# Mixer of a two-layer encoder kernel: jobs in another order, sixteen gate columns kept in DRAM

## The reference, cut to what matters

```python
for layer in range(2):
    xn = rmsnorm(h, mix_norm_g[layer])
    hq, hf, hi, hg, aq, ak, av, iq, ik, iw, gate_a, gate_b = split(xn @ w_in[layer])
    y_a = hgrn2_mixer(hq, hf, hi, hg, ...)       # 4 heads of 128, gated recurrence
    y_b = dsa_mixer(aq, ak, av, iq, ik, iw, ...) # 8 heads of 64, the best 132 keys of each query
    merged = sigmoid(gate_a) * (y_a @ w_branch_hgrn) + sigmoid(gate_b) * (y_b @ w_branch_dsa)
    h = h + merged @ w_out[layer]
    h = h + hier_moe(rmsnorm(h, ...))            # top-1 group, top-2 of its experts
return rmsnorm(h, final_norm_g)[:, 16:]
```

## Time and profile before

| what | value |
|---|---|
| median of three runs | 2030.24 us (2028.77 to 2033.95) |
| the profiled execution, its own time | 2032.07 us |
| its span | 2030.4 us |
| mean granted clock of TensorE | 0.845 of full speed |
| PE busy | 1575.7 us (78%) |
| DVE, ACT, POOL busy | 754.5, 543.2, 472.7 us |
| HBM read and written | 296.00 and 31.72 MB |

### The profile page before, as it was taken

How to read it: one execution, slowest core, us unless ns; L and a number is a source line. 1 busy time by engine, 2 the same in 40 slices (tenths; PEclk the granted TensorE clock), 3 DMA queues, 4 the chain that set the end, 5 groups by cost and what they waited for, 6 DMA issues and landing times.

```text
span 2030.4 us, 31814 instructions
## 1 busy us (share of the span) xinstructions
PE 1575.7 (78%) x11236; PEld 1193.3 (59%) x11236; DVE 754.5 (37%) x1772; ACT 543.2 (27%) x988; POOL 472.7 (23%) x349
## 2 busy tenths in 40 slices
PE   2998569967998597777459976799689986978771
PEld 2778349944976454444247863698379674545440
DVE  3018777944041311101241287696432223110103
ACT  3235432235221021111222444330543120111111
POOL 5312642100440010010143236230105101110002
PEclk9999559969998599989779975699589976999995
DMA  4224001210144199999832120011105343999995
GB/s 155 83 83 166 2 1 43 84 42 1 66 178 182 64 354 377 385 383 379 287 115 75 51 84 2 1 64 63 42 1 191 115 167 118 370 383 383 385 394 172
DMA packets 90628, 329.47 MB, mean 162 GB/s; under 512 B 10832, under 2 KB 11216, under 8 KB 73600
## 3 DMA queue, kind: packets, MB, share of 16 engines
q1 hardware_dynamic: 67536, 267.89, 35.2%
q0 software_dynamic: 9344, 33.95, 5.2%
q10 hardware_dynamic: 13616, 25.90, 3.6%
HBM read 296.00 MB, written 31.72 MB: 161 GB/s over the span
## 4 chain that ended last, share of the span: by engine, by line
PE 44%; issue 16%; SPq 15%; DMA 10%; DVE 8%; POOL 4%; ACT 3%; ACTq 0%; DVEq 0%; POOLq 0%
PE ps L585 14%; PE ps L608 12%; SPq L482 10%; SPq L487 4%; PE ps L850 4%; DMA gu_ring<-w_expert_up 3%; PE ps L595 3%; DMA r<-w_expert_up 3%; POOL gate_up_low L1754 2%; PE ps L776 2%; PE ps L871 2%; DMA r<-yrow,sidx 1%; PE ps L808 1%; PE ps L769 1%; PE ps L752 1%
## 5 line engine op out<-in xcount | busy, mean ns | idle before, releaser
L1754 POOL TENSOR_TENSOR gate_up_low<-gu_ring,chunk_high_a 128x1024 fp32r<-128x1024 f32 x80 | 193.1, 2434 | 531.6 <-ACT chunk_high_a L1486 531.6
L608 PE MATMUL ps<-x_high,gate_up_low 128*128 128x264 f32 (+1 forms) x928 | 265.5, 286 | 0.0
L608 PE MATMUL ps<-x_high,chunk_high_a 128*128 128x264 f32 x896 | 255.7, 285 | 3.5 <-POOL gate_up_low L1754 3.2
L608 PE MATMUL ps<-x_low,chunk_high_a 128*128 128x264 f32 x896 | 254.4, 284 | 0.0
L1817 POOL DMA_INDIRECT r<-xrow,idx x64 | 57.0, 890 | 663.0 <-PE ps L839 445.8
L608 PEld LDWEIGHTS ps<-x_high,gate_up_low 128*128 128x128 f32 (+1 forms) x928 | 173.4, 187 | 0.7
L850 PE MATMUL ps<-gu_ring,r 128*64 128x256 f32 x1024 | 131.3, 414 | 54.2 <-DMA gu_ring<-w_expert_up 52.9
L608 PEld LDWEIGHTS ps<-x_high,chunk_high_a 128*128 128x128 f32 x896 | 168.3, 188 | 5.4 <-issue 5.4
L608 PEld LDWEIGHTS ps<-x_low,chunk_high_a 128*128 128x128 f32 x896 | 168.5, 188 | 0.0
L585 PE MATMUL ps<-gate_up_low,x_high 128*128 128x512 f32 (+1 forms) x400 | 159.1, 398 | 0.0
L1388 DVE COPY r<-ps 128x512 f32<-128x512 f32 x64 | 44.2, 691 | 298.3 <-PE ps L839 298.3
(11 more groups left out here) (295 smaller groups left out, 3094.3 us busy)
## 6 DMA issues: line engine op xcount, KB each, us to landing
gu_ring<-w_in SPq DMA_DIRECT2D x20, 2048.0 KB, 8.3
gu_ring<-w_expert_gate SPq DMA_DIRECT2D x32, 1024.0 KB, 28.4
gu_ring<-w_expert_up SPq DMA_DIRECT2D x32, 1024.0 KB, 27.8
dn_ring<-w_expert_down SPq DMA_DIRECT2D x32, 1024.0 KB, 27.8
expert<-w_expert_gate SPq DMA_DIRECT2D x16, 1024.0 KB, 28.1
expert<-w_expert_up SPq DMA_DIRECT2D x16, 1024.0 KB, 27.2
expert<-w_expert_down SPq DMA_DIRECT2D x16, 1024.0 KB, 28.2
r<-w_expert_gate SPq DMA_DIRECT2D x16, 1024.0 KB, 28.6
```

The source lines that it names most:

```text
L608: last = mm(o[:, lo:hi], w[:, c, quarter(name, j)], x[:, c, lo:hi], start=c == 0 and k == 0, stop=c == KC - 1 and k == 2)
L1754: G.tensor_tensor(low[:, :, cols], w[:, :, cols], high[:, :, cols].bitcast(F32), ALU.subtract).then_inc(sem["part_low"], 1)
```

## The change

**Order of the jobs.** The index scores stand with the `hi` tiles and the `at` transposes, ahead of `hf`: one `hi` tile, eight `ix` jobs, the next `hi` tile and so on (`index_order`). Behind `hf` and `hq` come the eight columns of `ga`. The levels hold two columns of `gb` (after the level 4 of heads 0 and 2, `level_order`), two more `gb` columns follow the levels, and the last four `gb` columns and the eight `wa` columns stand in attention, one in each of the ten groups and two behind them (`FILL`). `hg` columns stand between the last states. `rope` is in two parts, the index part first.

**Selection.** All 17 rounds stand ahead of the levels on DVE, interleaved with `gate_in` and `gate_out`. ACT copies each `hf` column out of PSUM first (with scale -1), and `gate_in` reads that copy.

**Gate columns.** ACT copies each of the 16 gate columns out of PSUM into a ring of three (later into `osq`, now in AT's place) and writes it to a DRAM tensor `gates`, 264 KB each. After attention SP reads them back in four transfers of 1 MB, ACT takes four Sigmoids of 128x2112, and the merge has a fourth DVE operation for each column, since `wa` columns are now copied out of PSUM and multiplied by their gate in the merge.

**Others.** `hgrn_output` stands in attention's first four groups on DVE (one head each). The four high parts of `wo0` stand behind the Sigmoids on ACT. The load of expert 0 waits for the merge.

```diff
-CHUNKS = ["k3", "k2", "k1", "hi", "hf", "hq", "hg", "ga0", "ga1", "wa", "gb0", "gb1", "wb", "wo0", "wo1"]
+CHUNKS = ["k3", "k2", "k1", "hi", "hf", "hq", "ga0", "ga1", "gb0", "hg", "gb1", "wa", "wb", "wo0", "wo1"]
...
+GATES = [("ga", c) for c in range(8)] + [("gb", c) for c in range(8)]
+SLOT3 = 12
...
+def index_order():
+
+    yield ("hi", 0, 0)
+    for i in range(1, NT - 1):
+        for h in range(IH):
+            yield ("ix", i, h)
+        yield ("hi", i, 0)
+        if i == 1:
+            for k in range(NT):
+                yield ("at", k, 0)
+    yield ("hi", NT - 1, 0)
+    for h in range(IH):
+        yield ("ix", NT - 1, h)
...
+def level_order():
 
     for m in range(HH * LEVELS):
         yield ("lv", m // LEVELS, m % LEVELS)
-        if m % 2:
-            yield ("ix", 2 + m // 2 // IH, m // 2 % IH)
+        if m % 16 == 4:
+            yield (*GATES[8 + m // 16], 8 + m // 16)
...
+FILL = GATES[SLOT3:] + [("wa", c) for c in range(8)]
...
                         sp.wait_ge(*at("pe_done", JOBS[("pv", NT - 1, 1)] + 1))
+                        for s_ in range(4):
+                            sp.wait_ge(*at(f"gs{s_}", 64))
                         settle(sp)
-                        load_gate_up(0, 0)
-                        load_down(0, 0)
+                        for k in range(2):
+                            for dst, c0, name in ((sga, 0, "ga_in"), (sgb, 8, "gb_in")):
+                                sp.dma_start(dst[:, 4 * k:4 * k + 4, :], gates[:, c0 + 4 * k:c0 + 4 * k + 4, :]).then_inc(sem[f"{name}{k}"], 16)
+                sp.wait_ge(*at("mg_ready", 8))
+                sp.wait_ge(*at("pe_done", LAST["wb"] + 1))
...
+                for j in range(HH):
+                    if j == 0:
+                        select(0)
+                        done(("at", NT - 1))
+                    select(2 * j + 1)
+                    gate_in(j)
+                    select(2 * j + 2)
+                    gate_out(j)
+
+
+                for r in range(2 * HH + 1, rounds):
+                    select(r)
...
+                freed(("wa", 7))
                 for c in range(8):
-                    freed(("gb", c))
+                    dve.wait_ge(*at("sg_ready", 2 * (c // 4) + 2))
+                    link(tt(mrg[:, c, :], mrg[:, c, :], sga[:, c, :], ALU.mult))
                     done(("wb", c))
                     tt(sgb[:, c, :], wide(("wb", c)), sgb[:, c, :], ALU.mult).then_inc(*free(("wb", c)))
                     freed(("wb", c))
-                    tt(sga[:, c, :], sga[:, c, :], sgb[:, c, :], ALU.add).then_inc(sem["mg_ready"], 1)
+                    tt(mrg[:, c, :], mrg[:, c, :], sgb[:, c, :], ALU.add).then_inc(sem["mg_ready"], 1)
...
+                def gate_out(n):
+
+                    name, c = GATES[n]
+                    done((name, c))
+                    if 3 <= n < SLOT3:
+                        act.wait_ge(*at(f"gs{n % 3}", 16 * (n // 3)))
+                    settle(act)
+                    A(gate_row(n), wide((name, c)), ACT.Copy).then_inc(*free((name, c)))
+                    if n < 4:
+                        high_part("ga1", n)
+                    elif n < 8:
+                        high_part("gb0", n - 4)
+                    elif n < 12:
+                        high_part("hg", n - 8)
+                    freed((name, c))
+                    act.dma_start(gates[:, n, :], gate_row(n)).then_inc(sem[f"gs{n % 3 if n < SLOT3 else 3}"], 16)
...
+                for j in range(HH):
+                    done(("hf", j))
+                    A(hb[:, j, :], wide(("hf", j)), ACT.Copy, scale=-1.0).then_inc(*free(("hf", j)))
+                    high_part("hq", j)
+                    if j == 1:
+                        log_gates(0)
+                log_gates(1)
...
                 for q in range(4):
+                    low_part("gb0", q)
+                for kind, a_, b_ in level_order():
+                    if kind != "lv":
+                        low_part("hg", b_ % 4)
+                    elif b_ > 0:
+                        level_products(a_ * 7 + b_ - 1)
```

417 lines of the change are left out of this document (229 added, 188 removed).

## The result

| | median | runs |
|---|---|---|
| before | 2032.1 us | 2028.77 to 2035.82 (4) |
| after | 2086.8 us | 2082.57 to 2091.28 (4) |

The changed kernel takes 1.0269 times as long, with a 95% interval of 1.0239 to 1.0299. The direction is as forecast; the size is not: +54.7 us against +27, 1.8 us beyond the upper end of the range. The profiled execution took 2082.57 us, its span is 2080.9 us.

A forecast was written before the change was run, and what follows sets the result against it. PE bounds some stages, the chain DVE, ACT, POOL, PE others; the change trades between them. Stage terms, less the departed `wa`/`ga` stretch (-30.6) and `gb` (-47.0), sum to +13.4 us a layer: 2057 us, range 2012 to 2085.

The forecast's parts named there:

- D: Levels: index scores leave, two gate columns come in and each stalls the chain; +11 us a layer (bounds +1 and +21).
- The rival that PE would stall on ACT's list: From `hf` on, late ACT copies and high parts stall PE up to 10 us a layer; 2079 us, 0.12 shared with contention.
- C: Start of the levels: all selection rounds come first, so PE waits for DVE; +8 us a layer (bounds +2 and +16).
- H: End of attention to `wo`: gate reads, Sigmoids and a longer merge delay `wo`; +21 us a layer (bounds +10 and +28).
- F: States, `hg` and `on`: same work, so no change; 0 us a layer (bounds -6 and +2).
- B: Stages up to `hf`: all index scores move in among the `hi` tiles; +13 us a layer (bounds +10 and +20).
- G: Attention: four gate and six `wa` columns come in, partly hidden in PE's waits; +40 us a layer (bounds +24 and +58).
- E: Last level to first state: index accumulations go, masks and two `gb` columns come; -2 us a layer (bounds -5 and +3).
- rival 1: Levels, states and attention: PE filled more evenly is granted its upper clock, giving 24.5 us a layer; 2010 us, chance 0.23.

The follow-up runs named there:

- index_ahead: The kernel before with only the 32 index scores moved behind the transposes and ahead of `hf`, none in the levels: 2036.9 us, 1.0015 of before.

## Why the prediction was wrong

**Right.** The direction, the place of most costs, and D: levels without index scores 61 (61.2 measured), a stalled column 12.7 (12.4), sum +11 (+10.6, +9.4). The cheap fix that follows from it, moving the columns, gave its forecast. That the clock would not save the kernel was right for the levels (0.58, and 0.5 without the columns). The rival that PE would stall on ACT's list did not happen: PE is busy for 95.8 of the 96.5 us from `hf` to the last `ga` column.

**What failed, in one sentence.** The changed kernel lost more because three waits were priced too low or at nothing (C, H and F) and B was too short, while G, priced too high, gave more than half of that back.

**B, forecast +13, measured +16 and +21.** The step that failed was the sharing: I let a part of PE's index matmuls fill idle time, and PE's list had none, since it is busy for 115.6 of 117.9 us. Their own 18.0 us are near the 16 worked out, but by luck: the halving for the full clock is not what shortened them, as `index_ahead` shows with 18.0 us at 0.50. The 13 between the bounds 10 and 20 had no row behind it. The 3.5 us more in layer 1 are the lower clock in two `hi` tiles, which the term does not contain.

**C, +8, measured +16 and +19.** DVE's list was the right cause. Two terms were short: it starts 6.5 us behind `hf`, not 3.5; and it takes 107.9 us, not 100.5. The prediction's own sum is also off: 3.5 + 100.5 less 94.6 is 9.4 us behind PE, not 10.6, and so +6 and not +8. The rows name one source for both, POOL's low parts. Of the last four index products of DVE two meet them: they take 6.79 us together, where one alone takes 0.77, and without that the list would start about 3 us behind `hf` (an estimate from these rows). In the list itself the low parts arrive in threes since ACT, waiting for DVE, releases them late, just as DVE is in `gate_out`. In layer 0 such operations come to 11 us (2.1 for L1122 once, 2.2 for L1123 three times, 1.1 for L1126 twice). The same had cost 3 us in the kernel before (0.35, 0.7 and twice 1.05), inside the 37.5 us that the prediction took over, so some 8 are new, about the 7.4 by which the list is longer. The Trainium skill, GPSIMD Engine Reference, Key points, says that POOL contends with VectorE instructions that run in a 2-port perf mode or have two SBUF inputs; the prediction weighed the second half of it, for the merge alone. Here L1122 has two inputs and was held up, which agrees. L1123 and L1126 have one and were held up too; whether they run in such a mode no row tells. That this is all of the excess is argued from the rows; no run takes the contention away.

**H, +21, measured +31.** The Sigmoids (1.96 us each), the landings once issued (16 to 18 us) and the merge from there were as worked out. What failed is a premise that the order would have shown: I let SP issue at the last `pv`, but the load in front of the reads waits for the last `wa` column, which the change puts 7 us behind attention. Together with the issue of the residual rows the reads start 11.7 us behind the last `pv`. The first landing at 16.5 us, behind 5.3 MB at 390 GB/s, leaves about 3 for that, and the difference is 9 of the 10. The experiment with the reads first removed 15.

**F, 0, measured +6.** The states wait for the writes of gate columns: ACT's first copy of state rows waits 5.7 us for `gates<-r`, and PE 6.2 us for the copy where it had waited 0.7 at most. I counted the writes' cost nowhere. No run takes this wait away. **E, -2, measured -6:** the stretch is shorter by as much as DVE's eight index products took (6.0).

**G, +40, measured +24.** Without columns attention is 95.5 us against 83.8, and PE's wait for the normalised rows is 29.4 us against 17.1, so DVE's `hgrn_output` cost 12, not 5. The columns cost 13, not 35: they filled 23.6 us of idle time instead of 18.5, and the term for the clock had the wrong sign, 8.2 us won where 9 were to be paid. That term alone is 17 us, the largest error of the sum. The granted clock of 0.92 is the sign that the prediction had set for its first rival. So rival 1 was half right, in attention alone, where it gave back 9 us and 17 came.

**The total.** The misses on the high side (B 5, C 9, H 10, F 6) outweigh those on the low side (G 16, E 4, D 1) by 10 us a layer, 20 for two. With the 3.5 us outside that makes up most of the 28 us of difference in how much was lost (54.7 against 27); the profiled execution, at 2082.6, is 4 us under the median of the runs, which is the rest. That the time lies only 1.8 us beyond the range of 2012 to 2085 is therefore luck in part: without G's error in the clock it would have been some 34 us more, if layer 1 is taken to be as layer 0.

## What to carry to other kernels

When work is moved into an engine's idle time, look up what stands behind it in every list that it touches, not only on the engine that computes it: here a POOL instruction in front of ready products cost 11 of the 25 us a layer of the two columns in the levels, and the place of four reads in SP's list 15. Place filler where its consumer is not in the critical chain, and ahead of a wait rather than inside a ring of dependent steps; 25 us a layer were won by moving two columns by a few jobs. Work that fills idle time in a stage with a low granted clock can shorten the other work there too: it did in attention, by more than the columns' own slowing, and not in the levels, where two columns raised the clock from 0.50 to 0.58 and cost 12.4 us each.
